# A reworked head, forget-gate scores in two stacked passes, and another order of two steps' slots in a hybrid attention, convolution and gating kernel

## The chip, the cores and the metric

The kernel runs on one core of one Trainium2 chip. The metric is the device time of one execution in microseconds, lower being better. TensorE (PE) multiplies, VectorE (DVE) and ScalarE (ACT) read its results from PSUM, GpSimd (POOL) works on SBUF only, and SyncE (SP) issues the weight loads.

## What is computed

The first block is the part that the change touches. It has two attentions of 16 heads over 528 tokens (16 meta tokens and 512 real ones); the second of them adds the cumulated log forget gate to the logits.

```python
u = rmsnorm(h, pre_norm_g)                       # h = meta_tokens ++ x, 528 x 1024
cq, ckv, k_pe, z_mla, fq, fk, fv, f_logit, z_fox, gate_a, gate_b = split(u @ w_in)
q, kv = rmsnorm(cq) @ w_uq, rmsnorm(ckv) @ w_ukv # latent attention ("mla"), rope on 32 dims
o_mla = attention(q_m, k_m, v_mla)
cum   = cumsum(log_sigmoid(f_logit + fox_forget_b))
# "fox" attention, head dim 64: logit[t,s] = q.k/8 + cum[t] - cum[s], causal, softmax in f32
o_fox = attention(fq, fk, fv, cum)
mixed = (sigmoid(gate_a) * (o_mla * silu(z_mla)) @ w_br_mla
       + sigmoid(gate_b) * (o_fox * silu(z_fox)) @ w_br_fox) @ w_out
h = h + rmsnorm(mixed)
```

A second block of two layers follows (gated convolution and pooling; GELU and chunked spatial gating; each with a gated convolutional feed-forward part). It takes the span from about 560 us on and is the same in both kernels.

## The kernel before

Every f32 product is made of f32r pieces: a number is split into a high part (HI) and a rest (LO), and TensorE adds up three passes, HI·HI, HI·LO and LO·HI (`PASSES`). Weights are split where they arrive: SP loads a unit of 128x1024 into `w_raw`, ACT casts its high part (`w_hi`, L296), POOL subtracts (`w_lo`, L307), and PE waits for that with `w_ready`. There are two unit buffers. `c`, `c+1`, `c+2` are the units of a step.

**The head.** `nat` holds x in four tiles of 128 tokens and the meta tokens. ACT squares and sums the x tiles (L424), DVE does the meta tokens (L508) and scales (`normalise`, L515 and L517), PE transposes (L620 the meta tokens, L628 x: 32 transposes), ACT and DVE split the result into `u` (L437, L539) while applying the gain `pre_g`. Gains and convolution weights come as rows into `stage`, 14 small DMAs, and are transposed by PE (L613, L615) and copied by DVE into `vec`. Then come the products of the head: forget gate and rope key (`halves`, L637), and `cq` and `ckv` (`product`, L336).

**The steps.** A step s has eight beats b. In beat b, PE makes the scores of one head and one block of 128 queries of pair s-1 (`pe_scores`, L736 and L743; beats 0 to 3 one head, 4 to 7 the other), then a part of the products of pair s (`parts[b]`), then the transposes of the probabilities of beat b-1 (`pe_transposes`, L753). DVE takes the row maximum (`dve_max`, L1189), ACT the exponential (`act_exp`, L983), DVE normalises (`dve_norm`, L1194 and L1197), ACT and DVE split the transposed probabilities (`act_p` L999, `dve_p` L1202). After the beats, PE multiplies by the values (`pe_values`, L776). Transposes of beat b wait for `dve_p` of beat b-1, since one PSUM bank holds both. Steps 1 to 7 have latent attention and latent products ("mla" steps), step 8 has latent attention and fox products, steps 9 to 15 are fox and fox ("fox" steps), step 16 is fox attention with the products of the gates. Steps 2 to 5 and 10 to 15 are in loops. Every engine has its own program, in written order, and semaphores join them.

In a mla step ACT also rounds rope (L1060) and q (L1050), and POOL makes the rope's rest (L1343). In a fox step the cumulated gate joins the scores as extra rows: `pool_rows` lays it into `q_t` and `k_t` by DMA from `forget_rows`, with constant rows from memsets (L1358), and all three passes are 97 rows high.

## Time and profile before

| | |
|---|---|
| time, median of 3 runs | 1813.12 us (1812.51 to 1813.47) |
| time of the profiled execution | 1813.01 us |
| its span, first to last instruction | 1811.3 us |
| PE busy | 1749.8 us, 97% |
| DVE, ACT, POOL busy | 926.3, 769.2, 367.8 us |

The span is what the engines' rows cover; 1.7 us of the time lie around it. PE's busy time is that of instructions that overlap in a pipeline, so it says that PE is rarely idle, not that it is at its peak.

### The profile page before, as it was taken

The numbers are of one execution on the slowest core, as the hardware profiler recorded it, in microseconds if no ns is written. First come the engines' busy times: TensorE is split into PE (matmuls) and PEld (weight loads), VectorE is DVE, ScalarE is ACT, GpSimd is POOL, SyncE is SP. The second block draws the span as 40 slices with busy tenths as digits, with TensorE's granted clock in tenths as the row PEclk, the third lists the DMA queues.
The fourth block names the chain that finished last, engine by engine and source line by source line (L and its number), as shares of the span: only waits on it lengthen the run. The fifth ranks groups of instructions, "written<-read, shape, count | busy, mean of one in ns | idle before, by whom it ended". The sixth has DMA issues, their size and how long they took to land.

```text
span 1811.3 us, 25404 instructions
## 1 busy us (share of the span) xinstructions
PE 1749.8 (97%) x8651; PEld 1459.3 (81%) x8651; DVE 926.3 (51%) x1718; ACT 769.2 (42%) x1341; POOL 367.8 (20%) x389
## 2 busy tenths in 40 slices
PE   6899999999999999889999999999999999999998
PEld 5787878999987888668878888888888788888886
DVE  4567664666564334476455555433346555555322
ACT  5567666555554223333343333322264433333222
POOL 4445356333330000220111111001003211111000
PEclk9999999999999999899999999999999999999998
DMA  4121121211213334223333333333232233333332
GB/s 120 52 55 38 54 55 49 59 52 55 59 47 93 93 94 144 76 59 99 94 93 93 93 93 93 99 119 96 93 93 70 82 105 93 93 93 98 90 97 86
DMA packets 282519, 150.12 MB, mean 83 GB/s; under 512 B 11791, under 2 KB 278034, under 8 KB 282450
## 3 DMA queue, kind: packets, MB, share of 16 engines
q1 hardware_dynamic: 281874, 148.95, 28.4%
q8 instruction: 41, 0.67, 0.2%
q0 software_dynamic: 544, 0.20, 0.1%
q14 instruction: 28, 0.23, 0.0%
q10 hardware_dynamic: 32, 0.07, 0.0%
HBM read 147.02 MB, written 2.16 MB: 82 GB/s over the span
## 4 chain that ended last, share of the span: by engine, by line
PE 83%; DVE 7%; ACT 5%; issue 3%; POOL 1%; SPq 1%; ACTq 0%; DMA 0%; DVEq 0%; POOLq 0%
PE ps L336 68%; PE ps L915 3%; PE ps L776 2%; PE ps L2248 2%; PE ps L753 2%; PE ps L736 1%; DVE arena_r L1232 1%; DVE ps L1189 1%; DVE arena_r L1202 1%; ACT arena_r L1070 1%; ACT tmp L983 1%; PE ps L637 1%; PE ps L743 1%; ACT w_split L296 1%; PE ps L787 1%
## 5 line engine op out<-in xcount | busy, mean ns | idle before, releaser
L336 PE MATMUL ps<-u,w_split 128*128 128x512 f32 x3888 | 927.0, 396 | 11.7 <-DVE u L1828 7.3
L336 PEld LDWEIGHTS ps<-u,w_split 128*128 128x128 f32 x3888 | 729.3, 189 | 179.6 <-issue 7.6
L307 DVE TENSOR_TENSOR w_split<-w_raw,w_split 128x1024 fp32r<-128x1024 f32 (+1 forms) x221 | 268.2, 1213 | 436.6 <-ACT w_split L296 436.6
L296 ACT CAST w_split<-w_raw 128x1024 fp32r<-128x1024 f32 (+4 forms) x321 | 288.7, 913 | 417.3 <-PE ps L336 382.6
L336 PE MATMUL ps<-arena_r,w_split 128*128 128x512 f32 x1824 | 417.3, 390 | 1.7 <-DVE arena_r L2388 1.7
L336 PEld LDWEIGHTS ps<-arena_r,w_split 128*128 128x128 f32 x1824 | 341.9, 188 | 74.1 <-DVE arena_r L2388 3.3
L307 POOL TENSOR_TENSOR w_split<-w_raw,w_split 128x1024 fp32r<-128x1024 f32 (+3 forms) x100 | 137.8, 1396 | 49.7 <-ACT w_split L296 37.2
L2168 POOL TENSOR_TENSOR tmp<-tmp 128x512 f32<-128x512 f32 x44 | 57.1, 1297 | 425.7 <-ACT tmp L2153 425.7
L983 ACT ACTIVATE tmp<-ps,stats 128x144 f32<-128x144 f32 (+3 forms) x128 | 69.3, 541 | 115.4 <-DVE stats L1189 114.5
L1677 POOL TENSOR_TENSOR tmp<-tmp 128x512 f32<-128x512 f32 x40 | 56.9, 1422 | 269.5 <-ACT tmp L1636 234.5
L915 PE MATMUL ps<-u,w_split 128*128 128x264 f32 x768 | 101.6, 285 | 0.6 <-POOL w_split L307 0.6
L915 PEld LDWEIGHTS ps<-u,w_split 128*128 128x128 f32 x768 | 97.4, 188 | 1.6 <-POOL w_split L307 1.0
L1381 POOL TENSOR_TENSOR tmp<-tmp,ones 128x48 f32<-128x48 f32 x128 | 37.4, 292 | 250.2 <-DVE tmp L1197 250.1
L1202 DVE TENSOR_TENSOR arena_r<-ps,arena_r 128x128 fp32r<-128x128 f32 (+3 forms) x128 | 62.4, 488 | 38.0 <-ACT arena_r L999 37.4
L1189 DVE CUSTOM_DVE_ANT_0 ps<-ps,tmp 128x144 f32<-128x144 f32 (+3 forms) x128 | 65.8, 514 | 29.2 <-issue 27.3
L999 ACT CAST arena_r<-ps 128x128 fp32r<-128x128 f32 (+3 forms) x128 | 54.6, 426 | 57.5 <-PE ps L753 57.1
L776 PE MATMUL ps<-arena_r 128*128 128x512 f32 (+3 forms) x384 | 72.0, 330 | 2.5 <-DVE arena_r L1202 2.5
L2153 ACT ACTIVATE tmp<-tmp,vec 128x512 f32<-128x512 f32 x44 | 31.8, 723 | 97.1 <-DVE tmp L2189 97.1
L753 PE MATMUL ps<-cst,tmp 128*128 128x128 f32 x320 | 56.9, 276 | 12.8 <-DVE arena_r L1202 11.2
L2189 DVE SCALAR_TENSOR_TENSOR tmp<-tmp,vec 128x512 f32<-128x512 f32 x88 | 65.9, 749 | 5.5 <-DVE tmp L2189 0.3
L1674 POOL COPY tmp<-tmp 128x512 f32<-128x512 f32 x6 | 4.3, 717 | 310.2 <-ACT tmp L1778 170.7
L776 PEld LDWEIGHTS ps<-arena_r 128*128 128x128 f32 x384 | 58.8, 189 | 8.9 <-DVE arena_r L1202 4.5
(250 smaller groups left out, 1491.0 us busy)
## 6 DMA issues: line engine op xcount, KB each, us to landing
w_raw<-in_w_in_dram SPq DMA_DIRECT2D x118, 256.0 KB, 3.1
w_raw<-in_w_ffn_gate_dram SPq DMA_DIRECT2D x88, 256.0 KB, 3.1
w_raw<-in_w_ffn_up_dram SPq DMA_DIRECT2D x88, 256.0 KB, 3.1
w_raw<-in_w_ffn_down_dram SPq DMA_DIRECT2D x64, 256.0 KB, 3.1
w_raw<-in_w_in_even_dram SPq DMA_DIRECT2D x32, 256.0 KB, 3.0
w_raw<-in_w_in_odd_dram SPq DMA_DIRECT2D x32, 256.0 KB, 3.1
w_raw<-in_w_ffn_down_dram SPq DMA_DIRECT2D x32, 192.0 KB, 2.7
w_raw<-in_w_br_mla_dram SPq DMA_DIRECT2D x16, 256.0 KB, 3.0
```

The lines of the kernel that those rows point to most:

```text
L296: ins = act.copy(dst, src)
L307: ins = dve.tensor_tensor(lo, r, hi, ALU.subtract)
L336: last = pe.matmul(out_ap, w_tile(c, ws, k - n0), moving(k, ms), start=start and n == 0, stop=stop and n == len(total) - 1, skip_group_che ...
L753: ins = pe.transpose(bank(B_T, j * P, (j + 1) * P), prob[:, b % 2, META + j * P:META + (j + 1) * P], ident)
L776: pe.matmul(bank(B_O, j * P, 512), v_t[:, par, vs, j, v_cols(hh)], p_t[:, hh, pp * NQ + j, j * P:512], start=hh == 0 and j == 0 and n == 0 ...
L915: ins = pe.matmul(bank(b, 0, HALF), w_tile(c + j, ws, k), u[:, k, ms, half * HALF:(half + 1) * HALF], start=k == 0 and n == 0, stop=k == K ...
L983: act.activation(probs(b), scored(b), ACT.Exp, bias=neg[:, b:b + 1], scale=-1.0, accum_out=rs[:, b:b + 1]) \
L1189: dve.tensor_tensor_reduce(out=scored(b), in0=scored(b), in1=mask, scale=1.0, scalar=3.0e38, op0=ALU.add, op1=ALU.min, accum_out=neg[:, b: ...
L1202: dve.tensor_tensor(lo, src, hi, ALU.subtract).then_inc(sem("p_split"), 1)
L1677: ins = pool.tensor_tensor(acc[:, 0, :], acc[:, 0, :], sq[:, n % 2, :], ALU.add)
L2168: pool.tensor_tensor(cnv[:, j, :], cnv[:, j, :], rbc[:, 0, :], ALU.mult) \
L2189: dve.scalar_tensor_tensor(out=cnv[:, j, :], in0=gpad[:, j, tap:tap + SEQ], scalar=ffn_vec(layer, tap, f), in1=cnv[:, j, :], op0=ALU.mult, ...
```

## The change

**1. Head.** The gain `pre_g` is now transposed alone and first, from a DMA of its own that ACT issues. The other vectors are transposed later, between the products of units PRO+1 and PRO+2, and DVE copies them after the rope key. SP issues the load of unit PRO+1 ahead of the vectors' small DMAs. ACT squares the meta tokens and x tiles 0, 1 and 3, and DVE squares tile 2 with one 128x1024 reduction. The gate's product takes its passes 0 and 1 first, and pass 2, which needs POOL's part, from k = 4 on.

**2. Fox scores.** Two passes. The first (`PACKED`) is 128 rows high: rows 0 to 63 of q are its high part and rows 64 to 127 a copy of it, and k has its high part over its rest. The second (`REST`) is 68 rows high: the rest of q against the high part of k, with four rows for the cumulated gate. The copies of q and k are SBUF to SBUF DMAs that POOL issues in beats 4 and 6.

**3. Order.** In fox steps DVE does its second half of k after `dve_p` of beat 6, not before. In mla steps the last piece of `z_fox` moves from beat 7 to behind the transposes of the meta probabilities. Step 0 now makes the parts k = 0 to 5 of its `z_fox` (before k = 0 and 1), 12 matmuls more, and step 1 only the parts 6 and 7. ACT's slots 3 and 4 of mla steps: q moves behind the next exponential, and the cast of unit c+2 behind `act_p`.

```diff
         def load_prologue(sp):
...
+            w_load(sp, PRO + 1, panel(w_in, W_CQ))
             dma_vectors(sp)
-            w_load(sp, PRO + 1, panel(w_in, W_CQ))
-            sp.wait_ge(sem("vec_tr"), 1)
...
         def dve_prologue(dve):
...
             normalise(0, NQ)
+            dve.wait_ge(sem("meta_t"), 1)
+            dve.tensor_copy(vec[:, 0:KT], bank(7, 384, 384 + KT)).then_inc(sem("vec"), 1)
             normalise(1, 0)
-            dve.wait_ge(sem("vec_tr"), 1)
-            dve.tensor_copy(vec[:, 0:N_VEC], bank(7, 0, N_VEC))
...
+            dve.wait_ge(sem("x_in2"), 16)
+            dve.tensor_tensor_reduce(out=junk2, in0=nat[:, 2, :], in1=nat[:, 2, :], scale=1.0,
+                                     scalar=0.0, op0=ALU.mult, op1=ALU.add, accum_out=ssx[:, 2:3]) \
+                .then_inc(sem("x_ms"), 1)
             for t in range(1, NQ):
                 normalise(t + 1, t)
...
         def pe_prologue(pe):
-            pe.wait_ge(sem("cst_in"), 16)
-            pe.wait_ge(sem("vec_in"), N_VEC_DMA)
-            pe.transpose(bank(7, 0, N_VEC), stage[0:N_VEC, 0, :], ident[0:N_VEC, 0:N_VEC])
...
+            pe.wait_ge(sem("cst_in"), 32)
+            pe.transpose(bank(7, 384, 384 + KT), stage_g, ident[0:KT, 0:KT]).then_inc(sem("meta_t"), 1)
...
+            product(pe, bank(2), PRO + 1, u_real).then_inc(sem("w_used"), 1)
+            vectors()
+            w_ready(pe, PRO + 2)
+            product(pe, bank(3), PRO + 2, u_real).then_inc(sem("w_used"), 1)
...
         def pe_scores(pe, pr, b, fox, par, turn):
...
-                    pe.wait_ge(sem(f"rows{par}"), 32 * turn + (0 if par else 32))
+                    pe.wait_ge(sem(f"rows{par}"), 96 * turn + (0 if par else 96))
...
+            if fox:
+
+                passes = [(q_t[rows, slot, part, i * P:(i + 1) * P], k_t[rows, slot, part])
+                          for part, rows in ((PACKED, slice(0, P)), (REST, slice(0, HD + 4)))]
...
-        FIRST_CARRIED = 2
+        FIRST_CARRIED = 6
...
                 pe_transposes_meta(pe, pr)
+                if gemm == "mla":
+                    parts[8]()
...
         def fox_v_transposes(pe, s):
 
             pe.wait_ge(sem("v_copied"), s - PAIRS + 1)
+            pe.wait_ge(sem("k_split"), s + 1)
...
             dve_p(dve, pr, 6)
+            if gemm == "fox":
+                dve_k(dve, s, gemm, par, 1)
             dve_p(dve, pr, 7)
...
+        def pool_double_k(pool, s, par):
+
+            slots = slice(2 * par, 2 * par + 2)
+            pool.dma_start(k_t[0:HD, slots, REST].bitcast(F32), k_t[0:HD, slots, PACKED].bitcast(F32)) \
                 .then_inc(sem(f"rows{par}"), 16)
```

How the instructions stand now shows in three places. The first is ACT in step 1, from the exponential of beat 3 (528 wide) to that of beat 5 (272 wide); the loop's mla steps have the same order. Before:

```order
L983 ACTIVATE tmp,stats<-ps,stats 128x528
L1060 CAST arena_r<-tmp 32x512 x2
L1050 CAST arena_r<-ps 64x512 x2
L999 CAST arena_r<-ps 128x3x128
L983 ACTIVATE tmp,stats<-ps,stats 128x144
L296 CAST w_split<-w_raw 128x1024
L999 CAST arena_r<-ps 128x4x128
L983 ACTIVATE tmp,stats<-ps,stats 128x272
```

The same place in the changed kernel, in which L1011 is the exponential, L1088 rope, L1078 q, L1027 the probabilities and L297 the weight's cast:

```order
L1011 ACTIVATE tmp,stats<-ps,stats 128x528
L1088 CAST arena_r<-tmp 32x512 x2
L1027 CAST arena_r<-ps 128x3x128
L1011 ACTIVATE tmp,stats<-ps,stats 128x144
L1078 CAST arena_r<-ps 64x512 x2
L1027 CAST arena_r<-ps 128x4x128
L297 CAST w_split<-w_raw 128x1024
L1011 ACTIVATE tmp,stats<-ps,stats 128x272
```

The three-block probabilities now come before q, and the weight's cast, which POOL's part of the unit waits for, comes last before the exponential of beat 5.

The second place is POOL in step 9, from the rows of the cumulated gate to the end of the step. L1381 are the copies of the meta columns, one in each beat. Before:

```order
L1363 DMA arena_r<-forget_rows 1x4x512 [waits forget_out,aug]
L1365 DMA arena_r<-forget_rows 1x16x132
L1381 TENSOR_TENSOR tmp<-tmp,ones 128x3x16 [waits pm_transposed,normed]
L307 TENSOR_TENSOR w_split<-w_raw,w_split 128x1024 [waits w_hi]
L1381 TENSOR_TENSOR tmp<-tmp,ones 128x3x16 [waits normed] x3
L307 TENSOR_TENSOR w_split<-w_raw,w_split 128x1024 [waits w_hi]
L1381 TENSOR_TENSOR tmp<-tmp,ones 128x3x16 [waits normed] x3
L307 TENSOR_TENSOR w_split<-w_raw,w_split 128x1024 [waits w_hi]
L1381 TENSOR_TENSOR tmp<-tmp,ones 128x3x16 [waits normed]
```

In the changed kernel, where L1425 are the meta columns, L308 the weights, L1404 and L1410 the copies of q and k, the stretch from the second weight unit on reads:

```order
L308 TENSOR_TENSOR w_split<-w_raw,w_split 128x1024 [waits w_hi]
L1425 TENSOR_TENSOR tmp<-tmp,ones 128x3x16 [waits normed,q_hi]
L1404 DMA arena_r<-arena_r 64x2x512
L1425 TENSOR_TENSOR tmp<-tmp,ones 128x3x16 [waits normed]
L1425 TENSOR_TENSOR tmp<-tmp,ones 128x3x16 [waits normed,k_hi]
L1410 DMA arena_r<-arena_r 64x2x528
L308 TENSOR_TENSOR w_split<-w_raw,w_split 128x1024 [waits w_hi]
L1425 TENSOR_TENSOR tmp<-tmp,ones 128x3x16 [waits normed]
```

The copy of k stands between the meta columns of beat 6 and the next step's weight unit.

The third place is PE at the start of step 9, beats 0 to 3. Before:

```order
L736 MATMUL ps<-arena_r 128x144 x3
L336 MATMUL ps<-u,w_split 128x512 x9
L736 MATMUL ps<-arena_r 128x272 x3
L336 MATMUL ps<-u,w_split 128x512 x9
L753 MATMUL ps<-cst,tmp 128x128
L736 MATMUL ps<-arena_r 128x400 x3
L336 MATMUL ps<-u,w_split 128x512 x6
L915 MATMUL ps<-u,w_split 128x264 x6
L753 MATMUL ps<-cst,tmp 128x128 x2
L743 MATMUL ps<-arena_r 128x264 x6
```

And in the changed kernel:

```order
L761 MATMUL ps<-arena_r 128x144 x2
L337 MATMUL ps<-u,w_split 128x512 x9
L761 MATMUL ps<-arena_r 128x272 x2
L337 MATMUL ps<-u,w_split 128x512 x9
L777 MATMUL ps<-cst,tmp 128x128
L761 MATMUL ps<-arena_r 128x400 x2
L337 MATMUL ps<-u,w_split 128x512 x6
L940 MATMUL ps<-u,w_split 128x264 x6
L777 MATMUL ps<-cst,tmp 128x128 x2
L768 MATMUL ps<-arena_r 128x264 x4
```

Each score has one matmul less, the last block of a head two, and the products between them are the same.

## Rows read from the trace of the kernel before

**Rows 1.** Timeline of the head: start, us, engine, line, instruction, count, idle before.

```profile
4.93 1.21 DVE L508 CUSTOM_DVE_ANT_0 big<-big 16x1024 f32<-16x1024 f32 x1 [3.89 <-DMA big<-in_meta_tokens_dram]
...
15.42 0.37 PE L613 MATMUL ps<-cst,tmp 83*128 83x83 f32 x1 [15.42 <-DMA tmp<-in_b_conv_ffn_dram]
...
16.98 5.33 PE L628 MATMUL ps<-cst,big 128*128 128x128 f32 x32
...
17.55 0.76 DVE L517 TENSOR_SCALAR big<-big,stats 128x1024 f32<-128x1024 f32 x1
...
21.59 3.58 ACT L437 ACTIVATE u<-ps,vec 128x512 fp32r<-128x512 f32 x6 [3.80 <-PE ps L628]
...
23.86 6.03 PE L637 MATMUL ps<-u,w_split 128*96 128x264 f32 x48 [1.55 <-DVE u L539]
```

**Rows 2.** Timeline of PE in step 1.

```profile
72.88 1.69 PE L821 MATMUL ps<-arena_r,w_split 128*128 128x264 f32 x6 [0.28 <-POOL w_split L307]
```

**Rows 3.** Timeline of PE in step 2, an mla step (102.8 to 132.5).

```profile
117.80 0.63 PE L753 MATMUL ps<-cst,tmp 128*128 128x128 f32 x4 [0.99 <-DVE arena_r L1202]
...
130.27 2.15 PE L776 MATMUL ps<-arena_r 128*128 128x512 f32 x12 [0.31 <-DVE arena_r L1202]
```

**Rows 4.** Timeline of ACT in step 2, beats 3 to 5.

```profile
114.12 1.25 ACT L1060 CAST arena_r<-tmp 32x512 fp32r<-32x512 f32 x2
115.39 1.18 ACT L1050 CAST arena_r<-ps 64x512 fp32r<-64x512 f32 x2
116.59 0.48 ACT L999 CAST arena_r<-ps 128x384 fp32r<-128x384 f32 x1
117.09 0.38 ACT L983 ACTIVATE tmp<-ps,stats 128x144 f32<-128x144 f32 x1
...
117.47 1.03 ACT L296 CAST w_split<-w_raw 128x1024 fp32r<-128x1024 f32 x1
118.47 0.59 ACT L999 CAST arena_r<-ps 128x512 fp32r<-128x512 f32 x1
119.39 0.49 ACT L983 ACTIVATE tmp<-ps,stats 128x272 f32<-128x272 f32 x1 [0.34 <-DVE stats L1189]
```

**Rows 5.** Timeline of DVE and POOL in step 2, beats 1 and 5.

```profile
108.51 0.36 DVE L1197 TENSOR_SCALAR tmp<-tmp,stats 128x272 f32<-128x272 f32 x1
...
118.58 2.40 POOL L307 TENSOR_TENSOR w_split<-w_raw,w_split 128x1024 fp32r<-128x1024 f32 x1
...
120.20 0.94 DVE L1197 TENSOR_SCALAR tmp<-tmp,stats 128x272 f32<-128x272 f32 x1
```

**Rows 6.** Stretches, of L736 and then of L743: start:end, us, PE busy (count).

```profile
371.40:400.40 29.00, 3.72 (x18) 2.80 (x19) 1.00 0.21 56
...
371.40:400.40 29.00, 1.96 (x12) 1.58 (x12) 1.00 0.21 56
```

**Rows 7.** Timeline of PE in a fox step.

```profile
376.33 0.79 PE L736 MATMUL ps<-arena_r 97*128 97x400 f32 x3
376.96 1.56 PE L336 MATMUL ps<-u,w_split 128*128 128x512 f32 x6
...
396.14 0.63 PE L753 MATMUL ps<-cst,tmp 128*128 128x128 f32 x4 [0.34 <-DVE arena_r L1202]
```

**Rows 8.** Timeline of POOL and DVE at the end of that fox step.

```profile
391.85 2.39 POOL L307 TENSOR_TENSOR w_split<-w_raw,w_split 128x1024 fp32r<-128x1024 f32 x1
...
394.12 0.49 DVE L1197 TENSOR_SCALAR tmp<-tmp,stats 128x528 f32<-128x528 f32 x1
394.54 0.86 DVE L1232 SCALAR_TENSOR_TENSOR arena_r<-ps,arena_r 64x264 fp32r<-64x264 f32 x2
395.43 0.56 DVE L1202 TENSOR_TENSOR arena_r<-ps,arena_r 128x384 fp32r<-128x384 f32 x1
```

**Rows 9.** Timeline of POOL: two DMA issues, of 8 and of 66 KB.

```profile
395.65 0.56 POOL L1363 DMA_DIRECT2D arena_r<-forget_rows  x1 [0.66 <-issue]
...
46.84 0.67 POOL L1371 DMA_DIRECT2D forget_rows<-arena_r  x1 [1.85 <-DVE arena_r L581]
```

More of the change, by code:

```diff
@@ L377, in dma_vectors @@
             rows = 0
[L378 to L379 removed]
+            for name, n in VEC_ROWS[1:]:
+                src = {"q_g": a["mla_q_norm_g"], "kv_g": a["mla_kv_norm_g"],
                        "post_g": a["post_norm_g"], "mix_g": a["norm_mix_2"], "ffn_g": a["norm_ffn_2"],
@@ L630, in pe_prologue, with vectors, halves @@
                         ins.then_inc(sem("x_tr"), 1)
-            def halves(c, banks, ks, width=P):
+            def vectors():
+                pe.wait_ge(sem("vec_in"), N_VEC_DMA)
+                n = N_VEC - KT
+                pe.transpose(bank(7, 0, n), stage[0:n, 0, :], ident[0:n, 0:n])
+                for layer in range(2):
+                    ins = pe.transpose(bank(7, 128 * (layer + 1), 128 * (layer + 1) + FFN_ROWS),
+                                       stage[0:FFN_ROWS, 1 + layer, :], ident[0:FFN_ROWS, 0:FFN_ROWS])
+                ins.then_inc(sem("vec_tr"), 1)
+            def halves(c, banks, ks, width=P, passes=(0, 1, 2)):
                 for k in ks:
-                    for n, (ws, ms) in enumerate(PASSES):
+                    for n in passes:
+                        ws, ms = PASSES[n]
                         for half, b in enumerate(banks):
@@ L709, in pe_scores @@
             slot = 2 * par + hh
-            rows = slice(0, 97 if fox else 96 + 32 * hh)
+            rows = slice(0, 96 + 32 * hh)
             if b == 0:
@@ L874, in first @@
             def first():
-                if isinstance(s, int) and s == 1:
-                    carried(*range(FIRST_CARRIED, 4))
                 k_and_meta()
@@ L886, in turn, with second @@
                 z_fox(0)
-            return [first, lambda: carried(4, 5, 6), middle, q_nope, lambda: z_mla(0, 1, 2), lambda: z_mla(3, 4, 5),
-                    turn, lambda: z_fox(1, 2, 3)]
+            def second():
+                carried(*range(FIRST_CARRIED if isinstance(s, int) and s == 1 else 4, 7))
+            return [first, second, middle, q_nope, lambda: z_mla(0, 1, 2), lambda: z_mla(3, 4, 5),
+                    turn, lambda: z_fox(1, 2), lambda: z_fox(3)]
         def products_fox(pe, s, c, kk=0, i=0):
@@ L1144, in act_step @@
                         act_z_carried(act, s, c, kk, i)
-                elif b == (4 if gemm == "mla" else 3):
+                elif b == 3 and gemm == "fox":
                     w_hi(act, c + 2, i, kk, "full")
@@ L1160, in act_step @@
                     act_p(act, pr, b - 1)
+                if gemm == "mla" and b == 4:
+                    w_hi(act, c + 2, i, kk, "full")
                 if gemm == "fox":
@@ L1230, in dve_k @@
                 dve.wait_ge(sem("k_hi"), s + 1)
-            for src, dst, cols in k_pieces(gemm, par)[2 * half:2 * half + 2]:
-                ins = dve.scalar_tensor_tensor(out=dst[:, LO, cols], in0=src, scalar=-1.0, in1=dst[:, HI, cols],
+            for hh, (src, dst, cols) in enumerate(k_pieces(gemm, par)[2 * half:2 * half + 2]):
+                low = dst[:, LO, cols] if gemm == "mla" else k_t[HD:P, 2 * par + hh, PACKED, cols]
+                ins = dve.scalar_tensor_tensor(out=low, in0=src, scalar=-1.0, in1=dst[:, HI, cols],
                                                op0=ALU.mult, op1=ALU.subtract)
```

114 lines of the change are left out of this document (63 added, 51 removed).

## The prediction

> **What bounds the kernel now.** I read the head's timeline first, then PE's waits step by step, then for each wait the engines behind it. PE is busy 97% of the span, so only two things count: PE work that goes away, and PE's waits. In the head PE does nothing until the last small DMA of the vectors lands at 15.42 us, although x was there earlier; from 16.98 it transposes without a break, and ACT's first evacuation at 21.59 follows [rows 1]. In the mla steps PE waits twice, 0.99 us ahead of the transposes of beat 3 and 0.31 us ahead of the second head's values [rows 3]; the others of steps 2 to 7 show the same pair. In a fox step it waits 0.34 us, ahead of the transposes of beat 7 [rows 7]. Each of these waits is for DVE's split of probabilities, and behind DVE stands ACT's cast or a normalisation that came late. So the question for each part is what DVE's and ACT's chain does when PE gets faster.
>
> **Head.** Added: the meta tokens are now squared by ACT and tile 2 by DVE. New order of DVE: meta tokens scaled at about 7.4, gains copied, tile 0 scaled by 9.3, the meta product to 9.6, then the new reduction, 1.21 us by the row of the same length [rows 1], to 10.9; then tiles 1, 2, 3 at 0.76 + 0.16 each [rows 1], the last at 13.8. PE transposes 32 blocks in 5.33 us, 1.33 a tile [rows 1]: tile 1 starts at about 12.0, tile 3 at 14.7. Before, tile 3 started at 16.98 + 4.0 = 21.0. So ACT starts 6.3 us earlier, at 15.3, and u and the gate's product follow, since the product (6.03 us for 48 matmuls [rows 1]) remains PE's own time: taking pass 2 late keeps POOL's part off the path. The vectors' transposes come back between two products, 0.7 us (the start of the meta transposes against 15.42, about). Head: **-5.6**, bounds -6.3 (they hide in a wait) and -4.6 (a load or the f chain comes late by 1).
>
> **Steps 0 and 1.** Twelve matmuls move into an idle stretch of PE in step 0. But step 1's first product waits for POOL's split of a unit, at 72.88 [rows 2], and still will. What is gained is 0.5 us in beat 1, where six matmuls fewer stand before the scores of beat 2; it is spent again by what follows. Step 1: **0**, bounds -1.7 and +0.8.
>
> **ACT's slots 3 and 4, mla steps.** The 0.99 wait goes: the cast L999 no longer stands behind q, and runs 1.2 us earlier (1.18 [rows 4]). But PE's wait is not the last one. Behind rope ACT now does L999 (0.48), the exponential (0.38 + 0.1), q (1.18), L999 (0.59), then the weight's cast (1.03): added to 115.39, with 0.1 of gaps, they end at 119.28, where the cast ended at 118.50 before [rows 4]. POOL's split of that unit waits for it and takes 2.40 [rows 5]: 119.38 to 121.78, not 118.58 to 120.98. The next exponential stays at about 119.4, so the normalisation of beat 5 again begins near 120.1, inside POOL's instruction. And there it is held: it took 0.94 us, against 0.36 for the same shape with POOL idle, and ended 0.16 after POOL [rows 5]. In the changed kernel it ends at 121.94, 0.8 later. The chain q, maximum 6, exponential 6, normalisation, v, maximum 7 has no slack after that: PE's transposes of beats 6 and 7 came within 0.2 of DVE's splits before, and the last values waited 0.31 [rows 3]. So the step gets 0.8 longer, and `z_fox`'s last piece, 0.7 us of PE, now stands where 0.31 of wait was and fills a hole of beat 7 no longer: +0.15 more. **+0.95 a step**, six steps, **+5.7**; bounds 0 (the hold is no longer than before) and +1.2.
>
> The Trainium skill (SBUF — State Buffer, "SBUF: two separate sides") says that DVE in its two-port mode and GpSimd share one port pair as an exclusive lock, so the loser is blocked for the whole instruction. The trace agrees in the pair 0.94 and 0.36. By a sharing of bandwidth, which it rejects, a longer overlap would cost nothing more and the mla steps would come out at about 0.
>
> **Fox scores.** One pass of three goes. The score matmuls of a step are busy 3.72 + 1.96 = 5.68 us [rows 6]; a third is 1.9, but the last of each group overlaps the next instruction (the 400 wide group is busy 0.79, and the next product starts 0.63 after it [rows 7]), the short groups more: I take **1.4 a step**, 0.9 of it before beat 7. The height of 128 or 68 rows in place of 97 costs nothing in PE time by the rows that I have (a guess; the bound is that it costs as much as a pass, and then nothing is gained). The order of `dve_p` and the second half of k on DVE takes 0.86 [rows 8] from in front of the transposes of beat 7. PE alone would thus gain 1.4 + 0.34 = 1.75 a step.
>
> **The copy of k.** POOL issues it behind the meta columns of beat 6, and the next unit's split is queued behind it. No row shows such an issue: those of 8 and 66 KB take 0.56 and 0.67 us [rows 9], this one is 270 KB over 64 partitions. Call it D. The lower bound is the smaller row, 0.56; by the slope between the rows (0.11 for 58 KB) it would be 0.67 + 0.39 = 1.06; and since it has more pieces than either, I let the upper bound be 1.7, the slope two and a half times over. I take 0.9, a little under the slope, because an issue is mostly fixed cost in both rows. The split, 391.85 to 394.24 before [rows 8], starts at 390.93 + D (the chain is 0.92 earlier) and ends at 393.3 + D. Before, the normalisation of beat 7 started at 394.12, 0.1 us before POOL was done, and was not held (0.49) [rows 8]. Now it starts near 393.2, POOL has the lead, and it ends 0.3 after POOL, at 393.6 + D. Then L1202 (0.56 [rows 8]) and the transposes of beat 7 at 394.35 + D, before 396.14: a gain of 1.8 - D, less 0.1 for a values wait. At D = 0.9 **-0.8 a step**, six loop steps **-4.8**; bounds 0 and -1.2 each. Step 9 starts behind ACT's silu of eight tiles and keeps its first 9 us: **-0.4**. Step 8 has three-pass scores but has the copy: **0**, bounds -0.4 and +0.8. In step 16 (no copy, chain of DVE) **-0.3**. The copy of q in beat 4 and the doubled row DMAs fall into POOL's idle time; the copy of k has from its issue to the next step's first scores 7 us to land (beat 7 and the values), and I take that as enough; without that cover PE would wait for the landing.
>
> The Trainium skill (DMA: Bandwidth & Descriptors, "Anatomy of one DMA — SWDGE (gpsimd) path") calls descriptor generation small, with many descriptors emitted before the cost shows. No row here tests that at this size. By it D would be 0.6, and the sum 2 us lower.
>
> **Sum.** -5.6 + 0 + 5.7 + 0 - 0.4 - 4.8 - 0.3 = -5.4. The profiled execution took 1813.0, the median is 1813.1, so nothing is corrected: **1807.6 us**. Its own range is 1802 to 1814.
>
> **Rivals.**
> 1. The mla slots do what PE's waits promise. For it: the wait of 0.99 is real and its cause is removed. Against: the hold above. If the hold only keeps its old end, the six steps are 0 and the time is 1801.9; if both waits are gained (1.3 a step, seven steps), 1813 - 5.6 - 9.1 - 5.5 = 1793. Chance 0.25, most of it at the first.
> 2. The fox steps get the full PE gain, because POOL's split falls behind the normalisation, or D is tiny. Six steps at -1.75 and step 9 at -1.3: 1801. For it: before, the two missed each other by 0.1 us. Chance 0.12.
> 3. Slower: the copy of k holds POOL for 2 us. It slows steps 8 to 15, one us for each of D: the sum crosses zero at D = 0.9 + 5.4/8 = 1.6, and gives 1816 at D = 2. For it: an issue of this size is unseen. Against: 58 KB more cost 0.11 only. Chance 0.08.
> 4. The head gives 3 us less, a load or the f chain being late: 1810.6. Chance 0.10.
> My forecast has 0.45.
>
> **Numbers.** Within 0.2%, 3.6 us, a measurement of this kernel can't be told from no change. The forecast lies 1.8 us below that border, so of its 0.45 I put 0.27 on faster, 0.15 on same, 0.03 on slower; rivals 1 and 2 are faster, 4 is mostly same, 3 mostly slower: faster 0.65, same 0.25, slower 0.10. The range reaches to rival 1's low side and to rival 3: 1797 to 1815.
>
> **What would show it.** PE's first transpose near 6 us and ACT's first evacuation near 15.3. In steps 2 to 7 no wait at beat 3, but a wait of about 1 us at beat 6, the beat 5 normalisation over 1.5 us, each step about 1 us longer. In fox steps a POOL issue of 0.9 us, the beat 7 normalisation held, each step 0.8 shorter. The prediction is wrong if the normalisation of beat 5 isn't held longer, or if D is far from 0.9.

## The result and the profile after

The changed kernel takes 1798.91 us (median of 4 runs, 1797.87 to 1802.5), the kernel before, run beside it on the same chip, 1812.97 (1812.51 to 1813.47): a ratio of 0.9931, 95% interval 0.9917 to 0.9944. That is 0.7% faster, and the interval stays well clear of no change. 1807.6 was predicted, 8.7 us too much; the range of 1797 to 1815 holds the result, the narrower range of the likeliest case (1802 to 1814) doesn't. The profiled execution is the slowest of the four, 1802.5 us, so the traces differ by 10.5 us of span where the medians differ by 14.1.

The head of the changed kernel, timelines of PE and of ACT (start, us, engine, line, instruction, count, idle before):

```profile
6.07 0.27 PE L620 MATMUL ps<-cst,tmp 8*128 8x8 f32 x1 [6.07 <-DMA tmp<-in_pre_norm_g_dram]
...
11.48 4.07 PE L631 MATMUL ps<-cst,big 128*128 128x128 f32 x24 [0.23 <-DVE big L518]
...
17.10 6.03 PE L650 MATMUL ps<-u,w_split 128*96 128x264 f32 x48 [1.55 <-DVE u L540]
22.97 5.71 PE L337 MATMUL ps<-u,w_split 128*128 128x512 f32 x24
28.51 0.23 PE L638 MATMUL ps<-cst,tmp 75*128 75x75 f32 x1
28.58 0.32 PE L640 MATMUL ps<-cst,tmp 88*128 88x88 f32 x2
28.68 5.80 PE L337 MATMUL ps<-u,w_split 128*128 128x512 f32 x24
...
14.82 3.58 ACT L443 ACTIVATE u<-ps,vec 128x512 fp32r<-128x512 f32 x6 [2.28 <-PE ps L631]
```

Against [rows 1], PE's first transpose comes at 6.07 instead of 15.42, ACT's first evacuation at 14.82 instead of 21.59 and the gate's product at 17.10 instead of 23.86. The vectors' three transposes stand between 28.51 and the product that starts at 28.68: they cost 0.2 us.

Step 2, an mla step, now from 98.08 to 128.27 (timelines of ACT, POOL, DVE and PE):

```profile
110.67 0.48 ACT L1027 CAST arena_r<-ps 128x384 fp32r<-128x384 f32 x1
...
111.54 1.16 ACT L1078 CAST arena_r<-ps 64x512 fp32r<-64x512 f32 x2
112.73 0.59 ACT L1027 CAST arena_r<-ps 128x512 fp32r<-128x512 f32 x1
113.21 1.05 ACT L297 CAST w_split<-w_raw 128x1024 fp32r<-128x1024 f32 x1
...
114.34 2.40 POOL L308 TENSOR_TENSOR w_split<-w_raw,w_split 128x1024 fp32r<-128x1024 f32 x1 [0.46 <-ACT w_split L297]
...
114.98 1.92 DVE L1228 TENSOR_SCALAR tmp<-tmp,stats 128x272 f32<-128x272 f32 x1
...
117.77 0.93 PE L337 MATMUL ps<-u,w_split 128*128 128x512 f32 x3 [0.77 <-DVE arena_r L1252]
...
122.09 0.52 PE L777 MATMUL ps<-cst,tmp 128*128 128x128 f32 x3 [0.96 <-DVE arena_r L1233]
```

The wait at beat 3 is gone. The normalisation of beat 5 starts 0.64 us into POOL's instruction and ends 0.16 after it: 1.92 us where it took 0.94 [rows 5]. This is what "the hold" means below: the instruction can't end before POOL's. Of the 0.98 more, half comes from its end, which lies 0.49 later in the step, and half from its start, which lies 0.49 earlier. PE waits in beat 6 for what stands behind it, 0.77 for q's second half and 0.96 for the probabilities.

A fox step, from 395.62 to 423.42 (timelines of POOL, DVE and PE, then the stretch with each engine's busy time, count and PE's granted clock):

```profile
415.14 0.64 POOL L1410 DMA_DIRECT2D arena_r<-arena_r  x1
415.80 2.40 POOL L308 TENSOR_TENSOR w_split<-w_raw,w_split 128x1024 fp32r<-128x1024 f32 x1
...
417.68 0.83 DVE L1228 TENSOR_SCALAR tmp<-tmp,stats 128x528 f32<-128x528 f32 x1
...
419.12 0.63 PE L777 MATMUL ps<-cst,tmp 128*128 128x128 f32 x4 [0.34 <-DVE arena_r L1233]
...
395.62:423.42 27.80, 27.46 (x196) 25.64 (x195) 18.05 (x59) 15.96 (x40) 12.73 (x17) 1.00 0.31 76
```

POOL's issue takes 0.64 us, the normalisation 0.83 instead of 0.49 [rows 8], and PE's wait is 0.34 as before [rows 7]. The copy of k has landed 3.1 us after its issue (the median of eight), so the 7 us that the prediction gave it are enough. Lengths below run from one step's first score matmul to the next one's:

| us | before | after | difference | predicted |
|---|---|---|---|---|
| start of step 1 | 70.22 | 63.84 | -6.4 | -5.6 |
| step 1 | 32.60 | 34.24 | +1.6 | 0 |
| steps 2 to 7 | 176.53 | 179.28 | +2.8 | +5.7 |
| step 8 | 31.72 | 31.72 | 0 | 0 |
| step 9 | 31.41 | 31.05 | -0.4 | -0.4 |
| steps 10 to 15 | 174.04 | 166.55 | -7.5 | -4.8 |
| step 16, to its last value matmul (L781, L805) | 24.89 | 24.61 | -0.3 | -0.3 |
| the rest of the span | | | -0.4 | 0 |

The rest of what divides the medians isn't in the steps. The executions of one kernel lay 1 to 8 us apart within a set of runs, so the experiments are read by their step lengths first, which repeat within 0.1 us, and by their medians second.

In step 1 PE's clock is seen to matter. PE's timeline there and the granted clock of a stretch (it is the figure after the busy times):

```profile
66.49 1.69 PE L845 MATMUL ps<-arena_r,w_split 128*128 128x264 f32 x6 [2.12 <-POOL w_split L308]
...
68.41 2.87 PE L811 MATMUL ps<-arena_r,w_split 128*128 128x512 f32 x6
...
65.20:72.00 6.80, 5.51 (x19) 4.93 (x20) 1.44 (x5) 0.47 (x2) 1.52 (x5) 0.50 0.29 77
```

For 6.8 us the granted clock is 0.50, which is 1.2 GHz; before it was so for 3.4. The same six matmuls of L811 took 2.87 us here and take 1.60 in step 2.

### The profile page after: what moved, and what is told of

It is laid out like the page before. It is cut to its first block, busy times and chain, and to the rows that moved or that the text cites. A ratio compares the mean times of both kernels' runs of the same rounds, so it can differ in the third digit from the quotient of the medians.

```text
span 1800.8 us, 25312 instructions
## 1 busy us (share of the span) xinstructions
PE 1740.9 (97%) x8572; PEld 1446.2 (80%) x8572; DVE 940.0 (52%) x1719; ACT 767.1 (43%) x1341; POOL 377.0 (21%) x415
## 4 chain that ended last, share of the span: by engine, by line
PE 80%; DVE 9%; ACT 5%; issue 4%; POOL 1%; DMA 0%; ACTq 0%; DVEq 0%; POOLq 0%
PE ps L337 66%; PE ps L940 3%; PE ps L800 2%; PE ps L2298 2%; DVE ps L1220 1%; PE ps L777 1%; ACT tmp L1011 1%; DVE tmp L1228 1%; DVE arena_r L1264 1%; ACT w_split L297 1%; PE ps L761 1%; ACT arena_r L1098 1%; PE ps L650 1%; PE ps L811 1%; DVE w_split L308 1%
## 5 line engine op out<-in xcount | busy, mean ns | idle before, releaser
L308 DVE TENSOR_TENSOR w_split<-w_raw,w_split 128x1024 fp32r<-128x1024 f32 (+1 forms) x221 | 268.2, 1214 | 436.0 <-ACT w_split L297 435.9
L297 ACT CAST w_split<-w_raw 128x1024 fp32r<-128x1024 f32 (+4 forms) x321 | 288.8, 914 | 417.5 <-PE ps L337 382.8
L308 POOL TENSOR_TENSOR w_split<-w_raw,w_split 128x1024 fp32r<-128x1024 f32 (+3 forms) x100 | 137.5, 1394 | 48.2 <-ACT w_split L297 42.5
L1011 ACT ACTIVATE tmp<-ps,stats 128x144 f32<-128x144 f32 (+3 forms) x128 | 69.4, 542 | 122.6 <-DVE stats L1220 121.6
L1425 POOL TENSOR_TENSOR tmp<-tmp,ones 128x48 f32<-128x48 f32 x128 | 37.6, 294 | 230.8 <-DVE tmp L1228 229.9
L1027 ACT CAST arena_r<-ps 128x128 fp32r<-128x128 f32 (+3 forms) x128 | 54.7, 428 | 48.2 <-PE ps L777 47.7
L1228 DVE TENSOR_SCALAR tmp<-tmp,stats 128x144 f32<-128x144 f32 (+3 forms) x128 | 66.9, 523 | 4.5
```

The costliest lines, as they stand in the source:

```text
L297: ins = act.copy(dst, src)
L308: ins = dve.tensor_tensor(lo, r, hi, ALU.subtract)
L1011: act.activation(probs(b), scored(b), ACT.Exp, bias=neg[:, b:b + 1], scale=-1.0, accum_out=rs[:, b:b + 1]) \
L1228: dve.tensor_scalar(p, p, ri[:, b:b + 1], None, ALU.mult).then_inc(sem("normed"), 1)
```

## The experiments

All start from the changed kernel but the ninth and tenth, which start from the one before. Mean mla step is that of steps 2 to 7 (29.42 before, 29.88 after), fox step that of steps 10 to 15 (29.01 and 27.76).

**e1_carried: the 12 matmuls of z_fox back in step 1**

```diff
-        FIRST_CARRIED = 6
+        FIRST_CARRIED = 2
...
             def first():
+                if isinstance(s, int) and s == 1:
+                    carried(*range(FIRST_CARRIED, 4))
                 k_and_meta()
...
             def second():
-                carried(*range(FIRST_CARRIED if isinstance(s, int) and s == 1 else 4, 7))
+                carried(4, 5, 6)
```

> The changed kernel, but step 0 makes only the parts k = 0 and 1 of its z_fox and step 1 makes k = 2 to 6 again, 12 matmuls back in step 1. Theory: step 1 took 34.24 us instead of 32.60 because PE ran dry there, 2.1 us ahead of the first product of the unit that POOL splits, and its granted clock then stood at half for 6.8 us instead of 3.4. With the 12 matmuls back as cover, the wait falls under 0.5 us, the half clock stretch is 3.4 us again, step 1 takes 32.6, and the kernel is 1.6 us faster than the changed one. Rival: the half clock comes from PE's idle time in step 0, which stays; then step 1 keeps the 6.8 us and has 12 matmuls more, 34.3 or longer, and nothing is gained.

1798.97 us (ratio 0.9934, 0.9921 to 0.9948). PE's timeline and the stretch at half clock:

```profile
64.16 0.89 PE L761 MATMUL ps<-arena_r 96*128 96x144 f32 x3 [3.49 <-issue]
64.85 2.85 PE L337 MATMUL ps<-u,w_split 128*128 128x512 f32 x6
...
62.70:69.40 6.70, 5.24 (x19) 4.69 (x20) 3.43 (x10) 3.14 (x11) 2.81 (x7) 0.50 0.23 56
```

The wait of 2.1 for POOL is gone and the half clock is still there, for 6.8 us, from 62.7, which is inside PE's 3.49 us of idle time at the end of step 0. The theory that the dry spot in step 1 makes the clock fall is refuted. Of the rival, the half clock stays, but step 1 isn't 34.3 or longer, and its cause isn't shown: PE is idle for the same 3.49 us in the kernel before, where the half clock lasts 3.4, and e2 below has the changed kernel's idle times (0.71 and 2.11 us) and no half clock in step 1 at all. Step 1 takes 33.60 and step 2 starts at 97.76 instead of 98.08, so the 12 matmuls are nearly neutral: what they leave empty in step 0 they fill in step 1.

**e2_slots: ACT's slots 3 and 4 in the old order**

```diff
-                elif b == 3 and gemm == "fox":
+                elif b == (4 if gemm == "mla" else 3):
                     w_hi(act, c + 2, i, kk, "full")
...
                     elif b == 3:
                         act_rope(act, s, par)
-                    elif b == 4:
                         act_q(act, s, c, gemm, par, kk, i)
...
-                if gemm == "mla" and b == 4:
-                    w_hi(act, c + 2, i, kk, "full")
```

> The changed kernel with ACT's slots 3 and 4 of the mla steps in the old order (rope, q, probabilities of beat 2; the cast of unit c+2 ahead of the probabilities of beat 3). z_fox's last piece stays behind the transposes of the meta probabilities. Theory of the prediction, with its size corrected: the new order costs 0.3 of the 0.46 us that a mla step grew, because the normalisation of beat 5 is held by POOL for 1.92 us instead of 0.94; undone, the normalisation is back near 0.94, the wait of 0.99 ahead of the transposes of beat 3 is back, steps 2 to 7 take 29.4 instead of 29.74, and the kernel is 1.8 us faster. Rival 1: the new order itself gains, and the 0.46 come wholly from z_fox's last piece: then the steps get longer, 30 us or more, and the kernel 1 to 3 us slower. Rival 2: neither matters, within 0.1 us a step.

1794.79 us (0.9907, 0.9893 to 0.9921). Timelines of POOL, DVE and PE in step 3 (124.87 to 154.18):

```profile
140.27 2.41 POOL L308 TENSOR_TENSOR w_split<-w_raw,w_split 128x1024 fp32r<-128x1024 f32 x1
...
141.89 0.94 DVE L1225 TENSOR_SCALAR tmp<-tmp,stats 128x272 f32<-128x272 f32 x1
...
139.49 0.63 PE L777 MATMUL ps<-cst,tmp 128*128 128x128 f32 x4 [0.99 <-DVE arena_r L1230]
```

The hold is 0.94 again and the wait at beat 3 0.99, and the steps take 29.41 on the mean, what they took before to 0.01. The new order of ACT costs the whole 0.47 us a step, more than the 0.3 that I gave it, and gains nothing on balance: the wait that it removes was worth less than those it makes. Both rivals are refuted. The median is 4 us below that of the changed kernel; between the traces 2.8 us are in steps 2 to 7 and 2.6 in step 1, where this kernel has no half clock.

**e3_zfox: the last piece of z_fox back in beat 7**

```diff
-                    turn, lambda: z_fox(1, 2), lambda: z_fox(3)]
+                    turn, lambda: z_fox(1, 2, 3)]
...
-                if gemm == "mla":
-                    parts[8]()
```

> The changed kernel with z_fox's last piece (k = 3, three matmuls of 512 columns, 0.7 us) back in beat 7 of the mla steps. Prediction: the piece fills a hole of beat 7, so that putting it back gains 0.15 us a step, 29.6 instead of 29.74, 1 us in all; a wait of about 0.3 us stands again ahead of the last values. Rival: its new place is worth what the wait was, 0.3 us a step, and the steps take 30.0, the kernel 2 us slower.

1798.51 us (0.9935, 0.9922 to 0.9948); mla steps of 29.76, 0.12 less, and a wait of 0.3 ahead of the last values. The prediction's 0.15 was right with ACT's new order. With the old one (e2) the piece in its new place costs nothing.

**e4_split7: POOL's part of the next unit behind beat 7 in fox steps**

```diff
                 if gemm == "fox" and b == 0:
+                    if isinstance(s, int):
+                        pool.wait_ge(sem("w_lo"), c + 1)
                     pool_rows(pool, s - PAIRS, par)
...
-                elif b == 6:
+                elif b == (7 if gemm == "fox" else 6):
                     w_lo(pool, nxt, i, kk, KINDS[nxt])
```

> The changed kernel, but in fox steps POOL makes the rest of the next step's unit behind the meta columns of beat 7 instead of beat 6, so that DVE's normalisation of beat 7 runs without it. Theory: that normalisation, 0.83 us in the changed kernel, takes 0.49 or less, the transposes of beat 7 lose their wait of 0.34 us, the split starts near 418.5 instead of 415.8 in the step from 395.62 and ends 2.5 us ahead of the next step's first product, and each of the fox steps takes 27.4 instead of 27.75: 2.5 us faster over seven steps. Rival: the split now ends too late, because the next step's product or the unit's next load waits for it: a wait of PE for POOL's split at beat 0, or for ACT's cast at beat 1 (the load that follows comes 2.7 us later), and the steps get longer.

1794.69 us (0.9908, 0.9894 to 0.9922). DVE's and POOL's timeline and the whole step as a stretch:

```profile
413.67 0.49 DVE L1228 TENSOR_SCALAR tmp<-tmp,stats 128x528 f32<-128x528 f32 x1
...
414.50 2.37 POOL L308 TENSOR_TENSOR w_split<-w_raw,w_split 128x1024 fp32r<-128x1024 f32 x1
...
391.63:419.11 27.48, 27.46 (x195) 25.64 (x194) 17.75 (x59) 15.94 (x40) 12.56 (x17) 1.00 0.32 78
```

PE is busy for 27.46 of 27.48 us, with no wait left; the step is 0.30 shorter, as expected. Nothing came late behind the later part.

**e5_both: e2 and e4 together**

> The changed kernel with the two edits that helped: ACT's slots 3 and 4 of the mla steps in the old order, and POOL's part of the next unit behind the meta columns of beat 7 in fox steps. They work in different steps, so the theory adds them up: mla steps at 29.7 and 29.3 by turns, fox steps at 27.45, 3 and 2.5 us of the span, a median near 1791 to 1792 and under both kernels. Rival: a part of what each brought was where TensorE's half clock fell, and the sum is less, 1794.

1790.77 us (0.99, 0.9883 to 0.9917): mla steps 29.41, fox steps 27.46, and the sum holds.

**e6_mid: the weight's cast first in slot 4**

```diff
                     elif b == 4:
+                        w_hi(act, c + 2, i, kk, "full")
                         act_q(act, s, c, gemm, par, kk, i)
...
-                if gemm == "mla" and b == 4:
-                    w_hi(act, c + 2, i, kk, "full")
```

> The changed kernel, but in slot 4 of the mla steps ACT casts the weight of unit c+2 first, right behind the exponential of beat 4, then q, then the probabilities of beat 3; the probabilities of beat 2 stay ahead of that exponential. Theory: two things stood against each other in the slots. Early probabilities of beat 2 take away PE's wait of 0.99 at beat 3; the late cast brings a wait of its own in beat 6 because POOL's part then holds the normalisation of beat 5. With the cast early, POOL is done by about 16.5 us of the step, before that normalisation (16.9), which takes 0.36 or 0.5, and the wait at beat 3 is gone as well: steps of 29.0 to 29.2 on the mean, 0.8 below the changed kernel, 5 us in all, and 2 us better than the old order. Rival: q is now 1.0 us later and DVE waits for it ahead of the maximum of beat 5, so that the chain gives back what was gained: 29.5 or more on the mean, as in the old order.

1793.75 us (0.9908, 0.9893 to 0.9924), mla steps of 29.34. POOL and DVE in step 3 (124.69 to 153.97):

```profile
137.00 2.65 POOL L1376 TENSOR_TENSOR arena_r<-tmp,arena_r 32x512 fp32r<-32x512 f32 x2 [0.32 <-ACT arena_r L1088]
...
140.05 2.39 POOL L308 TENSOR_TENSOR w_split<-w_raw,w_split 128x1024 fp32r<-128x1024 f32 x1
...
139.90 0.68 DVE L1251 TENSOR_TENSOR arena_r<-ps,arena_r 64x512 fp32r<-64x512 f32 x1 [1.51 <-ACT arena_r L1078]
...
141.86 0.74 DVE L1227 TENSOR_SCALAR tmp<-tmp,stats 128x272 f32<-128x272 f32 x1
```

The theory overlooked POOL's rope: it keeps POOL busy until 139.65, so the early cast brings POOL's part no further forward than 140.05, where it starts in the step as in the old order (e2), and the normalisation is still held, 0.74. The rival's wait for q is there too, 1.51 where the changed kernel has 0.56. The steps lie between the two forecasts.

**e7_split5: POOL's part of unit c+2 behind beat 5**

```diff
-                elif b == (4 if gemm == "mla" else 3):
+                elif b == (5 if gemm == "mla" else 3):
                     w_lo(pool, c + 2, i, kk, "full")
```

> The changed kernel, but in mla steps POOL makes its part of unit c+2 behind the meta columns of beat 5 instead of beat 4, ACT's order as changed. It takes POOL away from the normalisation of beat 5 with nothing else moved. Theory of the hold: that normalisation takes 0.36 to 0.5 instead of 1.92 and the second half of q follows 1.4 us earlier; PE's waits of 0.77 for q's split and of 0.96 ahead of the transposes of beat 5 go. But POOL's part now runs from about 115.8 to 118.2 (step from 98.08), and PE's first product of that unit stands at 117.8, so a wait of 0.3 to 0.5 for POOL takes their place: steps of 29.4 on the mean, as in the old order. Rival: the steps grew by ACT's order itself and not by the hold; then they stay at 29.9 on the mean or get longer by the new wait.

1793.0 us (0.9905, 0.989 to 0.992), mla steps of 29.11. DVE, POOL and PE in step 3 (124.73 to 153.75):

```profile
141.24 0.36 DVE L1228 TENSOR_SCALAR tmp<-tmp,stats 128x272 f32<-128x272 f32 x1
...
141.92 2.37 POOL L308 TENSOR_TENSOR w_split<-w_raw,w_split 128x1024 fp32r<-128x1024 f32 x1
...
144.35 0.97 PE L337 MATMUL ps<-u,w_split 128*128 128x512 f32 x3 [1.08 <-POOL w_split L308]
```

ACT's order is untouched and the normalisation takes 0.36. Both waits of beat 6 are gone, one of 1.08 for POOL has come, and the step is 0.77 shorter. This shows that the hold is what costs the time: with it gone ACT's new order is no burden. It isn't a comparison of the two orders, since the old one (29.41 in e2) still has its hold of 0.94, and the old order with POOL's part behind beat 5 was not run.

**e8_two: the copy of k in two DMAs**

```diff
-                    pe.wait_ge(sem(f"rows{par}"), 96 * turn + (0 if par else 96))
+                    pe.wait_ge(sem(f"rows{par}"), 112 * turn + (0 if par else 112))
...
-            slots = slice(2 * par, 2 * par + 2)
-            pool.dma_start(k_t[0:HD, slots, REST].bitcast(F32), k_t[0:HD, slots, PACKED].bitcast(F32)) \
+            for hh in range(2):
+                slots = slice(2 * par + hh, 2 * par + hh + 1)
+                pool.dma_start(k_t[0:HD, slots, REST].bitcast(F32), k_t[0:HD, slots, PACKED].bitcast(F32)) \
...
```

> The changed kernel with the copy of k in two DMAs of one head each, so that POOL issues twice behind the meta columns of beat 6. One issue took 0.64 us; by that, two take 1.2 to 1.3. Theory: the time in front of POOL's part counts in full, since that part holds the normalisation of beat 7: each fox step gets 0.55 to 0.65 longer (28.35), eight steps, 4.5 to 5 us. Rival 1: PE has slack there, only 0.3 of it shows: 28.0, 2 us. Rival 2: an issue is a fixed cost on top of something that goes with the bytes, so that two halves cost the same as one, and nothing changes.

1802.27 us (0.995, 0.9937 to 0.9964). POOL and DVE in the step from 397.37 to 425.57:

```profile
416.87 1.07 POOL L1411 DMA_DIRECT2D arena_r<-arena_r  x2
417.96 2.40 POOL L308 TENSOR_TENSOR w_split<-w_raw,w_split 128x1024 fp32r<-128x1024 f32 x1
...
419.41 1.25 DVE L1228 TENSOR_SCALAR tmp<-tmp,stats 128x528 f32<-128x528 f32 x1
```

Two issues of half the size take 1.07, not 1.2 to 1.3. From those 0.43 us more follow a normalisation 0.42 longer and fox steps of 28.19, 0.43 longer: what stands in front of POOL's part counts in full. Both rivals are refuted.

**e9_head: the head alone, on the kernel before**

> The kernel before with the new head alone (the gain first, the vectors late, tile 2 squared by DVE, the gate's passes in two parts); steps 0 to 16 as before. Theory: the head is worth what the first scores of step 1 moved in the whole change, 6.4 us, and steps 1 to 16 take what they took: the start of step 1 at 63.8, the kernel 6 to 6.5 us faster than before. Rival: a part of the 6.4 came from the 12 matmuls that the whole change moves into step 0, or the gain is lost again in step 1, where PE's clock is at half for some us; then under 5.

1803.75 us (0.9961, 0.9947 to 0.9976), 7.9 below the 1811.69 of its neighbour; the interval is 5 us wide. Step 1 starts at 63.06, all steps behind it take what they took before, within 0.4 us in step 1 and 0.1 in the others. The rival is refuted by that start, 7.2 us earlier, more than by the median. The parts of the head weren't run one by one.

**e10_fox: the fox part alone, on the kernel before**

> The kernel before with the fox part alone: the two stacked passes, the copies, and DVE's second half of k behind the probabilities of beat 6. Head and mla steps as before. Theory: fox steps 27.75 as in the whole change, 1.25 less each, step 9 0.35 less, step 8 the same, step 16 a little less: 8.3 to 9 us faster than before. Rival: the earlier steps shift when the weights' loads and the clock's low stretches fall, and what is seen is under 7.

1803.02 us (0.9959, 0.9943 to 0.9975), 8.7 less. Fox steps of 27.75, step 9 at 31.05, step 8 at 31.69, as in the whole change; steps 9 to 15 hold 7.9 of it. The rival is refuted. The gains of e9 and e10, less the 2.8 of the mla steps, add up to 13.8, near the 14.1 of the whole change.

**e11_best: early cast, rope behind beat 7, and e4's move**

```diff
                     elif b == 4:
+                        w_hi(act, c + 2, i, kk, "full")
                         act_q(act, s, c, gemm, par, kk, i)
...
-                if gemm == "mla" and b == 4:
-                    w_hi(act, c + 2, i, kk, "full")
...
-                    elif b == 4:
-                        pool.wait_ge(sem("pm_copied"), 8 * pr + 4)
-                        pool_rope(pool, s, par)
...
-                elif b == 6:
+                elif b == (7 if gemm == "fox" else 6):
                     w_lo(pool, nxt, i, kk, KINDS[nxt])
+            if gemm == "mla":
+                pool.wait_ge(sem("pm_copied"), 8 * pr + 8)
+                pool_rope(pool, s, par)
```

> The changed kernel with four moves: in mla steps ACT casts the weight of unit c+2 right behind the exponential of beat 4, POOL's rope (2.65 us) goes from beat 4 to behind the meta columns of beat 7, so that POOL can make its part of that unit 1.2 us earlier, and in fox steps POOL's part of the next unit stands behind the meta columns of beat 7. Theory: what costs time in the mla steps is a normalisation of DVE inside POOL's long instruction. The early cast alone left it 0.74 us long, since POOL was still busy with rope when the cast was done. Now POOL's part runs from 14.1 to 16.5 us of the step, the normalisation of beat 5 at 17.2 is free, as is that of beat 7, and rope has the time to the next step's first scores: mla steps of 29.0 and 28.7 by turns, fox steps 27.45, a median of 1787 to 1788. Rival 1: q is the bound there (DVE waits for it ahead of the maximum of beat 5, 1.5 us with the early cast), so the mla steps stay at 29.6 and 29.3, a median of 1790.5. Rival 2: rope behind beat 7 holds the first normalisations of the next step or its first scores wait for it, and the steps get longer than 29.7.

1789.51 us (0.9885, 0.9869 to 0.99), the lowest median, 22 us below the kernel before. POOL, DVE and PE in step 3 (123.97 to 152.83):

```profile
138.15 2.41 POOL L308 TENSOR_TENSOR w_split<-w_raw,w_split 128x1024 fp32r<-128x1024 f32 x1
...
139.18 0.69 DVE L1251 TENSOR_TENSOR arena_r<-ps,arena_r 64x512 fp32r<-64x512 f32 x1 [1.51 <-ACT arena_r L1078]
...
141.14 0.36 DVE L1227 TENSOR_SCALAR tmp<-tmp,stats 128x272 f32<-128x272 f32 x1
...
140.98 0.30 PE L777 MATMUL ps<-cst,tmp 128*128 128x128 f32 x1 [0.52 <-DVE arena_r L1232]
...
146.69 0.52 PE L777 MATMUL ps<-cst,tmp 128*128 128x128 f32 x3 [0.41 <-DVE arena_r L1232]
```

POOL's part ends before the normalisation, which takes 0.36. The mla steps take 28.97 on the mean, between theory (28.85) and rival 1 (29.45): the hold is worth 0.37 against e6, and PE's waits of 0.52 and 0.41 stay, the first of them behind the 1.51 for which DVE waits for q. Whether q's place or something else bounds the rest was not tried.

**e12_k_order: DVE's second half of k ahead of the probabilities of beat 6 again**

```diff
-                    elif b == 6:
-                        dve_k(dve, s, gemm, par, 0)
+                    elif b in (6, 7):
+                        dve_k(dve, s, gemm, par, b - 6)
             dve_p(dve, pr, 6)
-            if gemm == "fox":
-                dve_k(dve, s, gemm, par, 1)
```

> The changed kernel with DVE's second half of k in fox steps ahead of the probabilities of beat 6 again, as before the change; the two passes and the copies stay. Theory: in the changed kernel PE waits 0.34 us for those probabilities, so that what is put in front of them shows in full: the two instructions of k take 0.88, the wait grows to 1.2, the fox steps to 28.6, 0.85 more each, and of the 1.25 us that a fox step gained only 0.4 are left. So the two passes alone would have been worth little, and the order of DVE is what lets them count. Rival: k's second half holds back nothing that PE wants in time, as the score matmuls saved are PE's own work: the step stays under 28.0.

1807.3 us (0.9972, 0.9963 to 0.9982). DVE and PE in the step from 397.60 to 426.41:

```profile
420.51 0.87 DVE L1264 SCALAR_TENSOR_TENSOR arena_r<-ps,arena_r 64x264 fp32r<-64x264 f32 x2
421.41 0.56 DVE L1233 TENSOR_TENSOR arena_r<-ps,arena_r 128x384 fp32r<-128x384 f32 x1
...
422.12 0.63 PE L777 MATMUL ps<-cst,tmp 128*128 128x128 f32 x4 [1.35 <-DVE arena_r L1233]
```

PE waits 1.35, and fox steps take 28.79, 1.03 more; steps 8 and 9 each grow by 1.0 as well. Two passes of three with DVE's old order gain 0.2 of the 1.25 us. The rival is refuted. The new order of DVE without the two passes was not run; PE had only its wait of 0.34 to give there [rows 7], so the 1.25 need both together.

## Why the prediction was right and where it was off

The direction was right and so were most mechanisms. The cost of ACT's slots was taken too high and the gains of fox steps and head too low; these three errors point the same way. The growth of step 1, which was left out, takes 1.6 us of them back. That the result lies within the range is owed to the room that the range left for the prices of rivals 1 and 2; the mechanism of neither came.

- **ACT's slots, +0.95 a step: right in kind, measured +0.46.** This is the term that was mis-sized most. That removing PE's first wait would gain nothing, since POOL then holds the normalisation of beat 5, is shown by the 1.92, by e2 (undone, the 0.47 come back) and by e7 (POOL's part alone moved, the hold and its waits go, and the step is 0.77 shorter). The size came from a sum of busy durations on ACT plus gaps: 3.89 us from the end of rope to the end of the cast. It took 3.6 (110.67 to 114.26). Of the difference 0.11 is the probabilities, whose 0.59 us are followed after 0.48, 0.11 what was put in behind the exponential of 0.38, which is followed after 0.37, and the rest gaps that aren't there. The hold thus ended 0.49 later in the step than before, not 0.8, and the step grew by 0.46. The sign that was named, a normalisation of over 1.5 us, came at 1.92 against 1.84 by luck: its end was forecast 0.3 too late, and its start 0.4 too late. The 0.15 for z_fox measured 0.12 (e3).
- **Fox steps, -0.8: measured -1.25.** The formula 1.8 - D - 0.1 was a good one, its D wasn't: 0.9 was taken, 0.64 is the issue, which the prediction itself had named as a sign against it, and the 0.1 for a values wait didn't come up. PE's own saving, taken at 1.4, is 1.16 (busy for 28.62 us of a step before and 27.46 after). With D = 0.64 the formula puts the transposes of beat 7 at 23.54 us of the step, and they start at 23.50. e8 shows that D counts one to one, e4 that 0.3 of hold is left, e12 that 1.03 of the 1.25 go when DVE's old order comes back. The guess that 128 or 68 rows cost no PE time holds: two matmuls of 400 columns are busy for 0.61 us where three took 0.79 [rows 7]. The slope that I drew from issues of 8 and 66 KB was no slope: 4 KB take 0.50 to 0.59, 66 KB 0.68, 132 KB 0.53 and 264 KB 0.64.
- **The head, -5.6: measured -6.4.** The evacuation came 0.5 earlier than predicted, as DVE scaled the last tile from 12.39 to 13.14 and not to 13.8, and the vectors' transposes cost 0.2, not 0.7. With the head alone (e9) step 1 starts 7.2 us earlier, so nothing else in the change was needed for it. Over all kernels with the new head that start stood between 62.7 and 64.2 us, and two things ahead of step 1 differ between them: the 24 transposes take 3.3 to 4.7 us (3.32 in e9, 4.07 in the changed kernel, which is nearly all of the 0.8 between their starts), and a stretch of half clock of 3.4 us falls ahead of step 1 or doesn't (not in e4 and e5, nor in e10, whose old head is 1.2 us shorter than the same head before). Why they differ was not tried. Rival 4 didn't come.
- **Step 1, 0: measured +1.6.** A clock was no part of my argument. Between kernels whose step 1 is the same, but for z_fox's piece in e3, it took 32.8 to 33.0 where the half clock lasted 3.4 us (e3, e4, e12) and 34.2 where it lasted 6.8 (after, e8). So 1.3 of the 1.6 is clock, and some 0.3 the change. What decides whether the clock is halved there, and for how long, stays open (e1).
- **Steps 8, 9 and 16** came as predicted within 0.1 us, but step 8 by what cancels: in e4 it is 0.36 shorter, in e12 1.0 longer.
- **The rivals.** The second was the nearest by its price, 1801 us, and by no mechanism: a fox step gained 1.25, not 1.75, and the hold got longer, not shorter. The first is refuted in the mla steps. The third, a POOL issue of 2 us, is far off.

The Trainium skill (DMA: Bandwidth & Descriptors, "Anatomy of one DMA — SWDGE (gpsimd) path") calls descriptor generation small, and the 0.64 agrees with it; the value that the prediction worked out by it, 0.6, was the better one. Its rule of the exclusive port pair (SBUF — State Buffer, "SBUF: two separate sides") agrees as well in that the held instruction of DVE ends 0.16 us (272 columns) or 0.31 (528) after POOL's wherever it starts inside it, for 0.94 and 1.92, 0.83 and 1.25 us, and POOL's takes its 2.40 throughout. One that did nothing at all until then would end 0.36 or 0.49 after it, its time alone; the measured ends come 0.2 sooner, and no run shows why.

Together the terms give 9.8 us to the start of step 16; with step 16 and the rest they are the 10.5 of the spans, 5.1 more than forecast. The other 3.6 between the medians go with the granted clock of the executions. Of 48 executions of the kernel before beside the experiments, the 13 with a mean granted clock of 0.994 or more took 1808.5 us in the median, the 35 with 0.989 to 0.992 took 1812.0. The changed kernel's four split likewise: 1797.9 and 1798.3 at 0.995, 1799.5 at 0.992, and the profiled one 1802.5 at 0.991, against 1813.0 at 0.990 for the profiled one before. So at like clocks the change is worth 10 to 11 us, and its median of 1798.9 is partly luck of the clock.

## What to carry to other kernels

A wait of the bounding engine names the last wait of one chain; before a move is priced by it, follow what the move makes late, and look above all for an instruction of VectorE from SBUF to SBUF that would start inside a long one of GpSimd: here it ended only after GpSimd's. Cost a chain by start-to-start times from the trace, not by sums of durations. When matrix work is taken away, move what stands on the elementwise engines in front of the next transposes too: here the saved matmuls alone brought 0.2 us a step, and 1.25 with the move. And compare builds by the lengths of their steps, or by executions of like granted clock, before their medians.
